# Six adaptive norms and the attention maps: VectorE's work divided between VectorE and ScalarE

## The reference

```python
for layer in range(DEPTH_2):
    mod = (c_act @ ada_w[layer] + ada_b[layer])[:, None, :]
    sh1, sc1, g1, sh2, sc2, g2 = jnp.split(mod, 6, axis=-1)
    h = rmsnorm(x, norm_mix[layer]) * (1.0 + sc1) + sh1
    ...                      # even: sparse top-k + differential attention; odd: forgetting attention
    x = x + g1 * y
    h = rmsnorm(x, norm_ffn[layer]) * (1.0 + sc2) + sh2
    x = x + g2 * peer_ffn(h, ...)   # per token 128 of 16384 experts: gelu(h . u[e]) * gate, times v[e]
return rmsnorm(x, norm_final)
```

## Time and profile before

| | us |
|---|---|
| median of 3 runs | 2545.63 (2542.87 to 2547.36) |
| the profiled execution | 2567.19, span 2565.5 |

### The profile page before, as it was taken

How to read it: one execution, slowest core, us unless ns; L and a number is a source line. 1 busy time by engine, 2 the same in 40 slices (tenths; PEclk the granted TensorE clock), 3 DMA queues, 4 the chain that set the end, 5 groups by cost and what they waited for, 6 DMA issues and landing times.

```text
span 2565.5 us, 23369 instructions
## 1 busy us (share of the span) xinstructions
PE 1732.8 (68%) x7234; PEld 1200.4 (47%) x7234; DVE 1608.0 (63%) x3441; ACT 371.6 (14%) x979; POOL 1211.1 (47%) x1124
## 2 busy tenths in 40 slices
PE   7999699998987237665557667555776755255555
PEld 5887587887866213442245335325443532011112
DVE  3338515602142998669875955997595698766764
ACT  1012501101021022111111211011131101000001
POOL 1001001200000468657775764676577467777773
PEclk9899899999987667888788869878887977677778
DMA  8646447943423789999999999999999999899995
GB/s 290 194 159 226 140 134 265 370 148 114 130 84 124 249 290 346 388 356 380 354 375 409 357 354 364 360 338 354 404 336 349 359 345 354 302 396 352 388 347 231
DMA packets 210158, 757.93 MB, mean 295 GB/s; under 512 B 23036, under 2 KB 26248, under 8 KB 209800
## 3 DMA queue, kind: packets, MB, share of 16 engines
q0 software_dynamic: 161280, 587.27, 61.5%
q1 hardware_dynamic: 48344, 167.35, 18.8%
q10 hardware_dynamic: 432, 2.03, 0.2%
HBM read 755.50 MB, written 1.07 MB: 295 GB/s over the span
## 4 chain that ended last, share of the span: by engine, by line
PE 36%; DVE 24%; POOL 17%; issue 12%; another core or an unknown queue 5%; DMA 4%; ACT 2%; DVEq 0%; SPq 0%; ACTq 0%
PE psL L426 31%; POOL W L417 17%; DVE W L913 6%; DVE Z L848 4%; PE psO L426 2%; DMA W<-experts_v,crow 2%; PE psS L426 2%; DMA wring<-weights 1%; DVE N L848 1%; DVE bias L854 1%; DVE bias L1321 1%; DVE bias L1333 1%; DVE bias L1324 1%; DVE N L851 1%
## 5 line engine op out<-in xcount | busy, mean ns | idle before, releaser
L426 PE MATMUL psL<-W,con 128*128 128x512 f32 x1024 | 623.3, 759 | 527.0 <-ACT con L1441 321.0
L417 POOL DMA_INDIRECT W<-experts_u,crow x512 | 591.7, 1156 | 582.1 <-DVE crow L851 357.9
L913 DVE SCALAR_TENSOR_TENSOR W<-W,Z 128x1024 f32<-128x1024 f32 x512 | 613.0, 1224 | 186.8 <-DMA W<-experts_u,crow 131.4
L417 POOL DMA_INDIRECT W<-experts_v,crow x512 | 568.3, 1110 | 284.7 <-issue 145.4
L426 PE MATMUL psL<-N,wring 128*128 128x256 f32 (+1 forms) x3568 | 628.8, 338 | 94.8 <-DVE N L851 60.7
L426 PEld LDWEIGHTS psL<-N,wring 128*128 128x128 f32 x3568 | 561.4, 199 | 167.7 <-DVE N L851 64.2
L426 PEld LDWEIGHTS psL<-W,con 128*128 128x128 f32 x1024 | 230.8, 240 | 873.6 <-issue 565.2
L848 DVE SCALAR_TENSOR_TENSOR Z<-W,crow,Z 128x1024 f32<-128x1024 f32 x252 | 324.0, 1286 | 45.4 <-DMA W<-experts_v,crow 24.6
L401 POOL DMA_DIRECT2D W<-ada x96 | 50.9, 530 | 453.6 <-DVE W L1043 452.8
L1441 ACT ACTIVATE Z<-psL 128x128 f32<-128x128 f32 (+2 forms) x190 | 60.0, 320 | 644.1 <-PE psL L426 519.6
L1441 ACT ACTIVATE con<-con,crow 128x128 f32<-128x128 f32 x256 | 86.2, 391 | 378.6 <-DVE crow L854 262.0
(11 more groups left out here) (197 smaller groups left out, 1334.1 us busy)
## 6 DMA issues: line engine op xcount, KB each, us to landing
wring<-weights SPq DMA_DIRECT2D x311, 512.0 KB
W<-ada POOLq DMA_DIRECT2D x96, 512.0 KB, 5.9
W<-experts_u,crow POOLq DMA_INDIRECT x512
W<-experts_v,crow POOLq DMA_INDIRECT x512
W<-rel_rows SPq DMA_DIRECT2D x1, 1536.0 KB, 9.0
X<-x_dram ACTq DMA_DIRECT2D x1, 1024.0 KB, 5.9
out<-N SPq DMA_DIRECT2D x1, 1024.0 KB, 3.9
W<-rel_rows SPq DMA_DIRECT2D x1, 768.0 KB, 4.9
```

The lines of the kernel that those rows point to most:

```text
L417: pool.indirect_dma_start(W[:, slot * D:(slot + 1) * D], None, experts_u if kind == "u" else experts_v, bass.IndirectOffsetOnAxis(ap=idx[: ...
L426: return pe.matmul(o, l, r, start=first, stop=last)
L913: dve.scalar_tensor_tensor(out=row, in0=row, scalar=1.0, in1=h_t[T], op0=ALU.mult, op1=ALU.mult, accum_out=dots[:, col:col + 1]).then_inc( ...
```

## The change

1. **Adaptive norms** (norms 3 to 9). DVE makes one product N = X * rstd over all chunks (128x2048 for norm 3, 128x1024 for the others) and sets a new semaphore, `xr_ready`. ACT waits for it behind its root and makes eight Identity activations with a scale (`amul`) and a bias (`mod`) per feature, in place in N; the last sets `n_ready`.
2. **Attention maps.** `scale` on DVE becomes `factors`: only the reciprocal and the factors; it sets a new semaphore, `facs_ready`. The scaling of Pb goes to ACT as two Copy activations with a scale, behind the Exp of the next job.
3. **Outputs.** `take` goes from DVE to ACT, behind the scaling of job a and ahead of `turned_maps` of job a.

```diff
-            def norm(n, wcol, shift=None, dst=None, T=None):
+            def norm(n, wcol=None, dst=None, T=None):
...
                 dve.wait_ge(rstd_ready, n + 1)
+                if wcol is None:
+                    n3, x3 = ((tile_of(t, 0, KC, T) if T is not None else t[:].rearrange("p (c s) -> p c s", s=S))
+                              for t in (N, X))
+                    tt(n3, x3, rstd[:, 0:w][:, None, :].to_broadcast([P, KC, w]), ALU.mult).then_inc(xr_ready, 1)
+                    return
                 for k in range(KC):
                     m = stt(part(dst, k), part(X, k), wcol(k), rstd[:, 0:w], ALU.mult, ALU.mult)
...
-                if shift is not None:
-                    link(m)
-                    for k in range(KC):
-                        m = ts(part(dst, k), part(dst, k), mod[:, shift + k:shift + k + 1], None, ALU.add)
...
-                def scale(jb):
...
-                    for m in range(2):
-                        p_ = Pb[:, b, m * S:m * S + w]
-                        ins = ts(p_, p_, facs[:, b, m:m + 1], None, ALU.mult)
-                    ins.then_inc(p_ready, 1)
-
-                def take(jb):
-                    n, T = jb["n"], jb["T"]
-                    dve.wait_ge(o_ready, n + 1)
-                    for slot, rows, unit in jb["outs"]:
-                        ins = dve.tensor_copy(toks(AT, unit, T, rows), psO[rows, slot * P:(slot + 1) * P])
-                    ins.then_inc(o_copied, 1)
+                    ins.then_inc(facs_ready, 1)
...
@@ ScalarE
+                scaled[0] += 1
+                act.wait_ge(xr_ready, scaled[0])
+                for k in range(KC):
+                    x = chunk(N, k) if T is None else toks(N, k, T)
+                    m = f(x, x, ACT.Identity, scale=amul[:, mul * KC + k:mul * KC + k + 1],
+                          bias=mod[:, shift + k:shift + k + 1])
+                m.then_inc(n_ready, 1)
...
+                def scale(jb):
+                    n, T, b = jb["n"], jb["T"], jb["n"] % 2
+                    act.wait_ge(facs_ready, n + 1)
+                    for m in range(2):
+                        p_ = Pb[:, b, m * S:m * S + keys_of(T)]
+                        ins = f(p_, p_, ACT.Copy, scale=facs[:, b, m:m + 1])
+                    ins.then_inc(p_ready, 1)
...
                 for a, jb in enumerate(js):
                     if a + 1 < len(js):
                         exps(js[a + 1])
+                    scale(jb)
+                    if a:
+                        take(js[a - 1])
                     turned_maps(jb)
                     if kind == "nsa":
                         take_in2(in2_beside(a))
                     rows(1)
+                take(js[-1])
```

More of the change, by code:

```diff
@@ L992, in front, with factors @@
                     ts(mx[:, b, 2:4], mx[:, b, 0:2], -1.0, None, ALU.mult).then_inc(smax_ready, 1)
-                def scale(jb):
-                    n, T, b = jb["n"], jb["T"], jb["n"] % 2
-                    w = keys_of(T)
+                def factors(jb):
+                    n, b = jb["n"], jb["n"] % 2
                     dve.wait_ge(exp_done, n + 1)
-                    link(dve.reciprocal(facs[:, b, 0:2], sums[:, b, 0:2]))
+                    ins = dve.reciprocal(facs[:, b, 0:2], sums[:, b, 0:2])
+                    if any(f is not None for f in jb["fac"]):
+                        link(ins)
                     for m in range(2):
@@ L1019, in attention @@
                         front(js[a + 1])
-                    scale(jb)
-                    if a:
-                        take(js[a - 1])
+                    factors(jb)
                     if kind == "nsa":
@@ L1186, in _ @@
             link(m)
-            norm(3, lambda k: amul[:, k:k + 1], shift=0)
+            norm(3)
             tt(tiny[0:64, 0:2], vec[0:64, VEC["blam"]:VEC["blam"] + 4:2], vec[0:64, VEC["blam"] + 1:VEC["blam"] + 4:2],
@@ L1269, in peer @@
                 rows(1)
[L1270 removed]
+                norm(n, T=T)
                 before, first, second = BESIDE[l, T]
@@ L1383, in odd @@
                 rows(1)
-                norm(NORM[f"odd{T} mix"], lambda k: amul[:, 2 * KC + k:2 * KC + k + 1], shift=48, T=T)
+                norm(NORM[f"odd{T} mix"], T=T)
                 rows(6)
@@ L1473, in rows, with norm @@
                     stream["done"] = r + 1
-            def norm(n, waits, T=None, sq=N, within=0, after=0):
+            scaled = [0]
+            def norm(n, waits, T=None, sq=N, within=0, after=0, mul=None, shift=None):
                 w = S if T is None else P
@@ L1506, in exps, with take @@
                     ins.then_inc(exp_done, 1)
+                def scale(jb):
[5 more added lines that the diff above has]
+                    ins.then_inc(p_ready, 1)
+                def take(jb):
+                    n, T = jb["n"], jb["T"]
+                    act.wait_ge(o_ready, n + 1)
+                    for slot, part, unit in jb["outs"]:
+                        ins = f(toks(AT, unit, T, part), psO[part, slot * P:(slot + 1) * P], ACT.Copy)
+                    ins.then_inc(o_copied, 1)
                 def turned_maps(jb):
@@ L1579, in _ @@
             norm(2, outputs_of("mlp2"))
-            norm(3, [(final_chunk, k + 1) for k in range(KC - 1)] + [(n_ready, 3)])
+            norm(3, [(final_chunk, k + 1) for k in range(KC - 1)] + [(n_ready, 3)], mul=0, shift=0)
             act.wait_ge(lam_sum, 1)
@@ L1611, in peer @@
             def peer(l, T, n, name):
-                norm(n, outputs_of(name), T, within=1, after=1)
+                norm(n, outputs_of(name), T, within=1, after=1, mul=2 * l + 1, shift=l * 48 + 24)
                 sc8, _ = scratch(l, T)
@@ L1648, in odd @@
                 turns[0] += 2
-                norm(NORM[f"odd{T} mix"], [(turn_taken, TURNS_PEER[0, T])] * KC, T, after=1)
+                norm(NORM[f"odd{T} mix"], [(turn_taken, TURNS_PEER[0, T])] * KC, T, after=1, mul=2, shift=48)
                 for j in range(25):
```

7 lines of the change are left out of this document (3 added, 4 removed).

## The result

| | before | changed |
|---|---|---|
| median of timed runs, us | 2544.25 (2541.69 to 2547.36) | 2576.16 (2571.25 to 2580.66) |
| ratio | | 1.011, interval 1.0076 to 1.0144 |
| timed again on another chip, us | 2475.51 | 2505.82 |
| ratio there | | 1.0115, interval 1.008 to 1.015 |

The change makes the kernel slower by 28 us (1.1% of 2544.25; 19 to 37 by the interval). The direction was forecast; the size was +10. Since the first profiled execution of before lay 21.6 us above its timed median, before was profiled once more (2570.3 us, on a chip where its timed median is 2574.45).

A forecast was written before the change was run, and what follows sets the result against it. PE was taken to bound the first attention, the serial chain of engines the second, GpSimd's gather issues the stream. +14.9 ahead of the stream and -5 in it gave +10: 2545.6 to 2555.6 us, range 2538 to 2574.

The forecast's parts named there:

- rival D: First attention: PE's waits lower its clock in ten units, +17 us more (2573), or late diagonals cost alike; chance 0.11.
- First attention: Sixteen steps, 161 to 275 us: scaling on ScalarE, behind copies and Exp, makes PE wait; +9.0 us, between +8 and +12.
- Second attention: Eight steps, 752 to 780 us, before expert rows: nothing hides the longer chain through ScalarE; +5.9 us.
- Norm 3: Norm over all tokens, ahead of the second attention: one product and eight activations take about as long as before; +0.2 us.
- Tile norms: Six norms over 128 tokens: -0.1 to -0.2 us each, one of them ahead of the stream.
- First gather: Start of expert-row fetching: the costs ahead of it sum to +14.9 us and shift it by that.
- Stream: Three attentions and five norms during expert-row fetching: little of VectorE's freed 39 us reaches the end; -5 us.
- rival C: VectorE is the real limit in the stream and its 39 us come through whole: -24, 2522 us; chance 0.13.
- the 12 us: In the stream: removed VectorE scalings would otherwise have held GpSimd through the shared port; up to 12 us more gain.
- the tightest thing: From about 930 us: GpSimd's gather issues nearly fill the time, 50.1 of 50 and 89.5 of 90 us.
- The credit of 5 us: In the stream: VectorE's shorter 2.83 us wait behind even tile 1's attention and some freed norm time; -5 us.
- Rival B: The stream gives back 10 to 20 us through freed norm time and earlier slots: within 5 us of before; chance 0.18.

The follow-up runs named there:

- the norms alone: Kernel before with only the changed norms (one VectorE product, eight ScalarE activations), all maps and outputs on VectorE: ratio 1.0032, +8 us.
- The late map order there alone: Kernel before with only the three stream attentions' maps scaled and outputs copied on ScalarE, in the change's order, norms as before: ratio 1.0023.
- the early order: Changed kernel with ScalarE's scaling moved right behind the copy of transposed maps, ahead of in2 copies and the following Exp: ratio 1.0005 to before.
- ScalarE's extra work: Kernel before with ten unused small copies on ScalarE ahead of the transposed-map copy in each of 24 stream attention steps: ratio 1.0005.

## Why the prediction was right in direction and short in size

The range held by very little. 2545.6 times 1.011 is 2573.6, its upper end was 2574, and the changed kernel's own median (2576.16) lies above that. The end was drawn from rival D alone, ten slow units; the time got there by four slow units, costlier norms and a loss in the stream. That the two meet is luck.

**First attention, forecast +9.0: measured +15.1** (128.36 against 113.23 us from first to last transposition, on one chip). The steps came out as worked: 10.00, 6.55, 7.18 and 7.61 us where 10.0, 6.6, 7.2 and 7.6 stood. The mis-sized term is the clock, which the sum left at zero and rival D priced at +17 for ten slow units. Four units ran slow, at 5.41 us (one at 5.33) in place of 3.72: 1.69 each, +6.7. 15.1 - 6.7 = 8.4, the forecast's term. D was a true mechanism and belonged in the sum with a part of its price, since the earlier trace rows already showed a slow unit behind a wait. Before has slow units of its own: 5.41 and 5.11 us in its first profile, inside the 42.98 that the sum started from, and one in the profile compared here:

```profile
223.21 5.41 PE L427 MATMUL psL<-N,wring 128*128 128x256 f32 x16
```

So three of the four, 5.1 us, are what the change added.

**Second attention, forecast +5.9: measured +4.9** (28.19 against 23.31 us). Right.

**Norm 3, forecast +0.2: measured +2.1** in the norms alone, +1.4 in the changed kernel on its second chip. Wrong twice. The price of the activations was taken from rows with a scale alone (0.40 apart); with scale and bias they start 0.50 apart: 0.9 us. And PE started slower behind it, by 0.5 to 1.2 us. **Tile norms, forecast -0.1 to -0.2: measured +0.5** (product to PE 4.50 us, at 1088.53 to 1093.03, against 3.96), for the same reason: 3.19 us for eight, 0.40 apart in place of 0.29.

**First gather, forecast +14.9: measured +20.2.** The clock in the first attention accounts for +6.7 of the difference, the norms for +1.8 to +2.5, the rest of the two attentions for -1.6. That is 7 to 8 us where 5.3 were measured, within the 3 us by which a first gather moves.

**Stream, forecast -5: measured about +8, between -0.4 and +17.** The reason given holds in its main point: VectorE's time was no limit (on one chip 58 us less busy, 72 us more idle for rows; 20 us more work cost nothing). So rival C falls, and with it the 12 us that the reading of the Trainium skill (SBUF — State Buffer, Who interferes with whom) would have brought by freeing GpSimd of the removed scalings: on one chip GpSimd was busy 1139.55 us for the 1024 gathers, and 1143.97 with the scalings on VectorE. That a scaling ever delays an issue was not tested by itself. What I called the tightest thing, GpSimd's issues, is not alone in that: rows landing late lengthen the stretch with the same issues. The credit of 5 us for the shorter wait behind the attention and for the norms did not come; the best estimate has the other sign, though its interval just holds zero. Rival B falls as well. The skill's other sentence (the Trainium skill, Perfetto Trace Analysis, Optimizing Scalar/DVE Operations: offload to ScalarE where VectorE is saturated) would have needed a finer test: VectorE, busy 49.08 of 50 us in a part of the stream, was full there, and over the whole stream its work was still no limit.

**Open:** what the stream loses in the changed kernel. Five norms at +0.5 are 2.5 us of it. The late map order there alone is +6 (-1 to +13), while the early order is free within its interval; ScalarE's extra work (+1) was too short a delay to decide it. Each is smaller than these intervals can tell apart.

## What to carry to other kernels

Moving work to an idle engine costs by the place it gets in that engine's order, not by the engine's busy share: with all work on the same engines the kernel lost 28 us with the scaling behind the copies and the Exp that wait for PE, and 1 us (-7 to +9) with it ahead of them. Before pricing such a move, ask when its input is ready, and put it right there. In a stretch where the transfers were busy 0.98 of the time, the work taken from VectorE turned into waiting for rows.

## What the runs showed of the hardware

- PE's clock: with waits of about 1 us in every step, the same sixteen fp32 matmuls of 256 columns took 3.72 us in most steps and 5.41 in some; with the waits gone none behind the first step was slow. After 9.22 us of idle time the granted clock in a window of 7 us was 0.54 (1.2 GHz would be 0.50, 2.4 GHz 1.00), after 8.35 us 0.72; after 6.68 us the first unit still came fast in one profile (5.21 us) and slowly in three (6.32 to 6.33).
- ScalarE: activations with a scale and a bias per partition start 0.50 us apart at 256 columns and 0.40 at 128; with a scale alone 0.40 and 0.29. Ten activations of one column start 0.09 us apart.
- Chips differ: before's median lay between 2475 and 2574 us from group to group. The first gather came within 3 us in five profiles, so the difference lies behind it: the same 1024 gathers took 1595 us on one chip and 1676 on another. The DMA engines' busy time accounts for 29 of those 81 us (0.98 of 1595, 0.95 of 1676); the cause of the rest is open.
